# A gated linear attention layer inside a decoder trunk: score blocks over three key tiles instead of chunk states, and a mean square made in one product

## The reference

```
log_a = jax.nn.log_sigmoid(gz @ w_gate_up + b_gate) / 16
b = jnp.cumsum(to_chunks(log_a), axis=3)                # within chunks of 64 tokens
b_ref = b[:, :, :, CHUNK // 2], b_last = b[:, :, :, -1]
scores = einsum('nbhik,nbhjk->nbhij', q * exp(b - b_ref), k * exp(b_ref - b)), causal
o_intra = scores @ v
state = exp(b_last) * state + (k * exp(b_last - b)).T @ v     # from chunk to chunk
o_inter = (q * exp(b)) @ state
o = o_intra + o_inter
o = o * rsqrt(mean(square(o)) + eps) * norm_w; y = o * silu(g); out = y @ w_out
```

## Time and profile before

| | us |
|---|---|
| median of 3 runs | 1059.52 (1059.49 to 1060.53) |
| the profiled execution, device time | 1059.4 |
| its span (first to last instruction) | 1057.7 |
| PE busy | 1038.2 (98%) |
| DVE busy | 728.3 (69%) |
| ACT busy | 521.0 (49%) |
| POOL busy | 131.7 (12%) |

### The profile page before, as it was taken

The page is one execution under the profiler, slowest core; times in us unless marked ns, Lnnn a source line. Parts: engine busy times, 40 slices in busy tenths (PEclk is TensorE's granted clock), DMA queues, the critical chain, the costliest instruction groups (busy, mean ns, idle before and its releaser), DMA issues.

```text
span 1057.7 us, 19726 instructions
## 1 busy us (share of the span) xinstructions
PE 1038.2 (98%) x8195; PEld 1020.7 (97%) x8195; DVE 728.3 (69%) x1100; ACT 521.0 (49%) x758; POOL 131.7 (12%) x146
## 2 busy tenths in 40 slices
PE   7999999999999999999999999999999999999996
PEld 6999999999999999999999999999888999999995
DVE  6765556689789755566796565768745899656644
ACT  4644335465356543344564344447855675444432
POOL 3000002320002000013300000222230220000132
PEclk9999999999999999999999999999999999999997
DMA  7865555637763856556467665662833538765631
GB/s 224 238 196 169 171 165 168 192 98 211 210 176 87 250 172 175 164 165 184 126 197 203 178 173 155 177 172 75 218 92 90 156 95 243 212 183 170 179 92 40
DMA packets 343722, 175.58 MB, mean 166 GB/s; under 512 B 6658, under 2 KB 342576, under 8 KB 343632
## 3 DMA queue, kind: packets, MB, share of 16 engines
q1 hardware_dynamic: 342992, 173.36, 57.6%
q10 hardware_dynamic: 448, 0.85, 0.2%
q0 software_dynamic: 192, 0.10, 0.0%
HBM read 173.24 MB, written 1.05 MB: 165 GB/s over the span
## 4 chain that ended last, share of the span: by engine, by line
PE 93%; DVE 2%; issue 2%; ACT 1%; DMA 1%; POOL 1%; SPq 0%; POOLq 0%; DVEq 0%
PE bank L1209 28%; PE bank L1211 28%; PE bank L1210 28%; PE bank L1234 2%; PE bank L1236 2%; PE bank L1235 2%; DMA raw_weights<-in_ffn_w_in_dram 1%; PE bank L1411 1%; PE bank L1428 1%; ACT weights_hi L427 1%; PE bank L1424 0%; DVE weights_lo L746 0%; PE bank L1437 0%; DVE rstd L862 0%; PE bank L1216 0%
## 5 line engine op out<-in xcount | busy, mean ns | idle before, releaser
L746 DVE TENSOR_TENSOR weights_lo<-raw_weights,weights_hi 128x1024 fp32r<-128x1024 f32 x335 | 415.6, 1246 | 227.3 <-ACT weights_hi L427 226.8
L427 ACT ACTIVATE weights_hi<-raw_weights 128x1024 fp32r<-128x1024 f32 x337 | 355.7, 1059 | 429.7 <-PE bank L1211 372.2
L1209 PE MATMUL bank<-x_hi,weights_hi 128*128 128x272 f32 (+1 forms) x1640 | 474.4, 289 | 0.9 <-ACT kT L629 0.8
L1211 PE MATMUL bank<-x_hi,weights_lo 128*128 128x272 f32 (+1 forms) x1640 | 472.6, 288 | 0.0
L1210 PE MATMUL bank<-x_lo,weights_hi 128*128 128x272 f32 (+1 forms) x1640 | 471.1, 287 | 0.0
L1209 PEld LDWEIGHTS bank<-x_hi,weights_hi 128*128 128x128 f32 x1640 | 310.4, 189 | 4.8 <-issue 2.2
L1211 PEld LDWEIGHTS bank<-x_hi,weights_lo 128*128 128x128 f32 x1640 | 310.6, 189 | 0.0
L1210 PEld LDWEIGHTS bank<-x_lo,weights_hi 128*128 128x128 f32 x1640 | 310.5, 189 | 0.0
L1211 PE MATMUL bank<-mid_hi,weights_lo 128*128 128x272 f32 (+1 forms) x704 | 202.0, 287 | 0.0
L1209 PE MATMUL bank<-mid_hi,weights_hi 128*128 128x272 f32 (+1 forms) x704 | 201.5, 286 | 0.0
L1210 PE MATMUL bank<-mid_lo,weights_hi 128*128 128x272 f32 (+1 forms) x704 | 201.1, 286 | 0.0
(11 more groups left out here) (186 smaller groups left out, 905.1 us busy)
## 6 DMA issues: line engine op xcount, KB each, us to landing
raw_weights<-in_ffn_w_in_dram SPq DMA_DIRECT2D x176, 512.0 KB, 3.9
raw_weights<-in_ffn_w_out_dram SPq DMA_DIRECT2D x64, 512.0 KB, 3.8
raw_weights<-in_ffn_w_out_dram SPq DMA_DIRECT2D x32, 384.0 KB, 3.4
raw_weights<-in_conv_w_in_dram SPq DMA_DIRECT2D x24, 512.0 KB, 3.9
raw_weights<-in_gla_w_in_dram SPq DMA_DIRECT2D x24, 512.0 KB, 3.9
raw_weights<-in_conv_w_out_dram SPq DMA_DIRECT2D x8, 512.0 KB, 4.7
raw_weights<-in_gla_w_out_dram SPq DMA_DIRECT2D x8, 512.0 KB, 4.0
out_dram<-out_tok SPq DMA_DIRECT2D x3, 256.0 KB, 2.2
```

The lines of the kernel that those rows point to most:

```text
L427: nc.scalar.activation(w_hi[:, n % RING, :], raw[:, n % RAW, :], ACT.Copy).then_inc(hi_split, 1)
L746: nc.vector.tensor_tensor(w_lo[:, s, :], raw[:, n % RAW, :], w_hi[:, s, :].bitcast(F32), ALU.subtract).then_inc(lo_split, 1)
L1209: nc.tensor.matmul(ps, w_h, hi[:, k, cols], start=first and k == k0, stop=False)
L1211: mm = nc.tensor.matmul(ps, w_l, hi[:, k, cols], start=False, stop=last and k == k1 - 1)
```

## The change

The chunk states are gone. Tokens are counted in four chunks of 64 from the first meta token (BEFORE = 256) and a rest of 16. Three tiles of keys (128, 128 and 16) meet the queries behind them directly: eight small float32 products make one head's scores (`scores`), with keys that carry the decay to the end of their chunk (`k_late`, POOL, with a second copy one chunk further by DVE) and queries that carry more decay (`q_late`, two small DVE instructions; `late_decays`). Three products per half of the values make the outputs. `turn_k`, `copy_k`, `outers` and `states` are removed. `scores(h)` stands at j = 11 + 2h as before, `outputs(h)` one tile earlier, at 12 + 2h. `decays(h)` stands one tile earlier on ACT.

The mean square is one product with a full 128x128 matrix, so its result stands on all partitions and `spread_rms` is gone. DVE first adds the two halves of the squares (`sum_squares`). Roots and reciprocals are made per head. The last two gate products are on DVE. The four gate logits are made after tile 4, in the middle of tile 5, after it, and in the middle of tile 6, in banks 0 to 3, and tiles 5 and 6 no longer wait for earlier copies.

```diff
 # ACT
-                if j in (9, 11, 13, 15):
-                    decays((j - 9) // 2)
-                if j in (13, 15, 17, 19):
-                    copy_o((j - 13) // 2)
-                if j in (18, 20):
-                    root_ms((j - 18) // 2)
+                if j in (8, 10, 12, 14):
+                    decays((j - 8) // 2)
+                if j in (12, 14, 16, 18):
+                    copy_o((j - 12) // 2)
+                if j == 17:
+                    root_ms(0, 2)
+                    root_ms(2, 1)
+                if j == 19:
+                    root_ms(3, 1)
 # POOL, apply_decays (k_st, q_pos, kT, qT before)
+                nc.gpsimd.tensor_tensor(k_late[:, h % 2, :, 0:3:2, :], k_main, by_last, ALU.mult).then_inc(kst_ready, 1)
...
+                nc.gpsimd.tensor_tensor(q_pos[:, h, :], qT[:, h, :], e_buf[:, 0, META:T], ALU.mult).then_inc(decayed, 1)
...
+                nc.gpsimd.tensor_tensor(qT[:, h, :], qT[:, h, :], e_buf[:, 2, META:T], ALU.mult).then_inc(decayed, 1)
...
+                nc.gpsimd.tensor_tensor(kT[:, h, :], kT[:, h, :], e_buf[:, 1, :], ALU.mult).then_inc(decayed, 1)
-            for m in range(KD):
+            for m in range(KD - 2):
                 gate_output(m)
 # DVE
+            def late_decays(h):
+                dve.wait_ge(exps_ready, 5 * h + 5)
+                dve.wait_ge(kst_ready, h + 1)
+                nc.vector.tensor_tensor(k_late[:, h % 2, :, 1, :], k_late[:, h % 2, :, 0, :],
+                                        decay[:, h, 1:NC:2].rearrange("p (a o) -> p a o", o=1).broadcast_to([P, NC // 2, CH]),
+                                        ALU.mult).then_inc(late_ready, 1)
+                dve.wait_ge(decayed, 3 * h + 2)
...
+                nc.vector.tensor_scalar(q_late[:, h % 2, :], qT[:, h, SEQ - LATE:SEQ], decay[:, h, 2:3], None,
+                                        ALU.mult).then_inc(late_step, 1)
+                dve.wait_ge(late_step, h + 1)
+                nc.vector.tensor_scalar(q_late[:, h % 2, CH:LATE], q_late[:, h % 2, CH:LATE], decay[:, h, 3:4], None,
+                                        ALU.mult).then_inc(late_ready, 1)
+            def sum_squares(h):
+                dve.wait_ge(o_squared, h + 1)
+                if h >= 1:
+                    dve.wait_ge(ms_made, h)
+                nc.vector.tensor_tensor(o_sum[:], o_sq[:, 0, :], o_sq[:, 1, :], ALU.add).then_inc(o_summed, 1)
...
                 if j < GLA_TILES - 1:
                     split_lo(n0 + j + RING)
...
-                if j in (7, 9, 11, 13):
-                    differences((j - 7) // 2)
+                if j in (7, 8, 10, 12):
+                    differences((7, 8, 10, 12).index(j))
+                if j == 8:
+                    nc.vector.memset(sT[:, :, 0, 0:META], 0.0).then_inc(margin_set, 1)
+                if j in (10, 12, 14, 16):
+                    late_decays((j - 10) // 2)
+                if j in (13, 15, 17, 19):
+                    sum_squares((j - 13) // 2)
                 if j in (11, 13, 15, 17):
                     copy_scores((j - 11) // 2)
                 if j == 18:
                     invert_rms(0)
+                    scale_o(0)
+                    invert_rms(1)
+                if j == 19:
+                    scale_o(1)
+                    invert_rms(2)
                 if j == 20:
                     scale_o(2)
+                    invert_rms(3)
                     scale_o(3)
-        Y_CHUNKS = {21: (0, 1), 22: (2, 3), 23: (4, 5), 24: (6, 7)}
+        Y_CHUNKS = {20: (0, 1), 21: (2, 3), 22: (4,), 23: (5,), 24: (6, 7)}
 # PE, scores(h): keys x queries, M x N
+                pe.wait_ge(decayed, 3 * h + 3)
+                pe.wait_ge(late_ready, 2 * h + 2)
+                product(kT[:, h, 0:P], 0, q_pos[:, h, 0:P - META])                                  # 128 x 112
+                product(late[:, 0, 0:CH], CH - META, qT[:, h, CH - META:P - META])                  # 64 x 64
+                product(late[:, 0, CH:3 * CH], P - META, qT[:, h, P - META:P - META + CH])          # 128 x 64
+                product(late[:, 0, CH:3 * CH], P - META + CH, q_late[:, h % 2, :])                  # 128 x 80
+                product(kT[:, h, P:2 * P], SEQ, q_pos[:, h, P - META:2 * P - META])                 # 128 x 128
+                product(late[:, 1, 0:CH], SEQ + CH, qT[:, h, P - META + CH:2 * P - META])           # 64 x 64
+                product(late[:, 1, CH:3 * CH], SEQ + P, qT[:, h, BEFORE - META:SEQ])                # 128 x 16
+                product(kT[:, h, BEFORE:T], SEQ + P + REST, q_pos[:, h, BEFORE - META:SEQ]).then_inc(scores_made, 1)  # 16 x 16
 # PE, outputs(h): per half of the values 256, 144 and 16 columns
+                    nc.tensor.matmul(bank[3][:, first:first + SEQ], v_tok[:, h % 2, 0, v_cols], sT[:, h % 2, 0, META:T],
+                                     start=True, stop=False)
...
 # PE, mean_square(h)
+                pe.wait_ge(o_summed, h + 1)
+                nc.tensor.matmul(bank[1 + h // 2][:, h % 2 * SEQ:(h % 2 + 1) * SEQ], meanV[:], o_sum[:],
+                                 start=True, stop=True).then_inc(ms_made, 1)
...
-                pe.wait_ge(gla_evac, j - 3 if j < 7 else j - 2 if j < 12 else j - 1)
+                if j >= 7:
+                    pe.wait_ge(gla_evac, j - 2)
...
+                middle = (lambda: logits(1)) if j == 5 else (lambda: logits(3)) if j == 6 else None
...
+                if j in (12, 14, 16, 18):
+                    outputs((j - 12) // 2)
+                if j in (11, 13, 15, 17):
+                    scores((j - 11) // 2)
+                if j in (13, 15, 17, 19):
+                    mean_square((j - 13) // 2)
+            pe.wait_ge(gla_evac, GLA_TILES - 1)
```

More of the change, by code:

```diff
@@ L229, in tokens @@
             return slice(T - n, T)
[L232 to L241, removed]
-        def tile_bank(j):
[L244 to L253, removed]
+        def tile_bank(j):
+            return 4 + (j - 3) % 3
         block = ctx.enter_context(nc.Block())
@@ L1137, in invert_rms @@
-            def invert_rms(part):
-                heads = slice(0, 96) if part == 0 else slice(96, P)
-                dve.wait_ge(rms_root, part + 1)
-                nc.vector.reciprocal(rms[heads, :], rms[heads, :]).then_inc(rms_ready, 1)
+                across = SEQ + BEFORE - P + REST
+                dve.wait_ge(margin_set, 1)
+                nc.vector.tensor_copy(sT[:, h % 2, :, :].rearrange("p b t -> p (b t)")[:, META:META + across],
+                                      bank[0][:, 0:across]).then_inc(scores_copied, 1)
@@ L1197, in block_of, with multiply @@
                 return w[:, n % RING, k * P:(k + 1) * P]
-            def multiply(ps, n, source, cols, k0=0, k1=KU, first=True, last=True, ready=None, before_last=None):
+            def multiply(ps, n, source, cols, k0=0, k1=KU, first=True, last=True, ready=None, before_last=None, middle=None):
                 hi, lo = source
@@ L1207, in multiply @@
                         before_last()
+                    if middle is not None and k == (k0 + k1) // 2:
+                        middle()
                     w_h, w_l = block_of(w_hi, n, k - k0), block_of(w_lo, n, k - k0)
@@ L1368, in _, with logits @@
             main = tokens(SEQ)
-            def logits(heads):
-                pe.wait_ge(gla_evac, 1)
+            def logits(h):
+                pe.wait_ge(gla_evac, h + 1)
                 pe.wait_ge(gate_landed, 32)
-                for h in heads:
-                    nc.tensor.matmul(bank[4 + h][:, 0:T], gate_up[:, h * P:(h + 1) * P], gzT[:], start=True,
-                                     stop=True).then_inc(logits_made, 1)
+                nc.tensor.matmul(bank[h][:, 0:T], gate_up[:, h * P:(h + 1) * P], gzT[:], start=True,
+                                 stop=True).then_inc(logits_made, 1)
@@ L1386, in turn_v, with scores @@
+                for b in range(BEFORE // P):
+                    mm = nc.tensor.transpose(bank[7][:, b * P:(b + 1) * P], vT[:, v % 2, b * P:(b + 1) * P], ident[:])
                 mm.then_inc(v_turned, 1)
-            def turn_k(h):
-                pe.wait_ge(kst_ready, h + 1)
+            def scores(h):
+                pe.wait_ge(decayed, 3 * h + 3)
+                pe.wait_ge(late_ready, 2 * h + 2)
+                pe.wait_ge(log_a_ready, 1)
                 if h >= 1:
-                    pe.wait_ge(state_ready, NC * h)
-                for b in range(BLOCKS):
-                    r = slice(0, META) if b == 0 else slice(META + (b - 1) * P, min(META + b * P, KT0))
-                    mm = nc.tensor.transpose(bank[4][0:r.stop - r.start, b * P:(b + 1) * P], k_st[:, h % 2, r], ident[:])
-                mm.then_inc(k_turned, 1)
@@ L1397, in scores @@
[L1397 to L1413 removed]
+                    pe.wait_ge(scores_copied, 2 * h)
@@ new lines, in scores, with product @@
+                ps = bank[0]
+                late = k_late[:, h % 2, :, :, :].rearrange("p a b i -> p a (b i)")
```

(5 more changed lines are left out.)

242 lines of the change are left out of this document (83 added, 159 removed).

## The result

| | before | changed |
|---|---|---|
| median of 6 runs, us | 1060.85 (1059.49 to 1062.18) | 1064.80 (1063.94 to 1068.50) |
| the profiled execution, device time | 1059.4 | 1064.0 |
| its span | 1057.7 | 1062.2 |
| PE busy | 1038.2 | 1033.4 |

The ratio is 1.0045, with a 95% interval of 1.0032 to 1.0059: slower, and clearly more than no change. (The two medians alone differ by 3.95 us, the means of the six runs by 4.7 and the fastest runs by 4.45.) PE has less to do and the kernel lasts longer. The page of the changed kernel shows both, against the earlier trace rows: 4.8 us less busy time, and a chain that lies less on PE (91% after 93%) and more on DVE (4% after 2%) and ACT (2% after 1%).

What follows compares the result with a forecast made beforehand. PE bounds the kernel, busy 98% of the span with 93% of the chain. Front 4.4, middle -1.9, tail 0 and clock 1.7 + 1.2 sum to +5.4 on 1059.4, giving 1064.8 us; range 1060.4 to 1067.0.

Steps and rivals of the forecast that it cites:

- Front, +4.4: Up to tile 12: waits for ACT's copy and DVE's `late_decays(0)` move its start from 762.16 to 766.6; bounds +2.9 to +5.2.
- half clock behind this stop would be hidden: Behind the stop before `turn_v(0)`: tile 11 runs partly at half clock but ends at 763.7, ahead of `scores(0)` at 765.0.
- Middle, -1.9: Tile 12 to the end of tile 18: 38.8 us against 40.7, with stops of 1.25 us at j = 13, 15 and 17.
- `outputs` with 256, 144 and 16 columns, twice, (0.43 + 0.25 + 0.20) x 2 = 1.76: PE's own work: time of the new `outputs` products per head, 1.76 us against the old 2.63.
- The prediction's last sentence: The forecast is wrong if differences or sum come earlier on DVE, or `scores` takes much over 1.9 us, costing in the middle.
- The rival in which the sum is not late: Middle and tail: DVE reaches the sum in time, stops (7.7 us) and half clock behind the last go; 1054.2, chance 0.10.
- Tail, 0: End of tile 18 to the end of `out_projection`'s first chunk: 29.75 us against 29.8; bounds -1.5 to +1.5.
- Clock, +2.9: Half clock after the j = 19 stop (+1.7) and after the first chunk (+1.2, between 0 and 1.7).
- both places that the prediction names: Half clock was forecast in tile 20, behind the 3.9 us stop at j = 19, and from `out_projection`'s first chunk into the next.
- Nearly sure: Tile 20: the 3.9 us stop at j = 19 is followed by half clock, +1.7 us.
- PE's work, 10.5 us less: Whole attention stage: 25.9 us of PE work removed, 4 x 3.85 added, so PE's work falls by 10.5 us.
- the prediction's lower bound of 1.35 us: `scores` per head: 1.35 us if narrow products take only a transpose's 0.11; 1.6 was taken, upper bound 1.67.

Runs made afterwards that it cites:

- e6: Changed kernel with the eight products of `scores` ordered by stationary width (five of 128 columns, two of 64, one of 16): 1066.33 us, ratio 1.0061.
- e1: Changed kernel with the sum of squares ahead of DVE's weight split (heads 0 to 2), head 3's at j = 18 ahead of the second reciprocal: 1060.66 us.
- e12: e4 with unused products as fillers: 2 before `turn_v(0)`, 5 before `turn_v(1)`, 4 before `scores(0)`; 1061.75 us, ratio 1.0021.
- e7: Changed kernel with the logits in two pairs after tiles 4 and 5 again, as before: 1067.17 us, ratio 1.0068.
- e9: e6 on top of e1: sum of squares moved and products grouped, nothing moved in front; 1058.55 us, ratio 0.9983.
- e8: Changed kernel with the moves of e1, e2 and e3 together and the grouped products of e6: 1058.27 us, ratio 0.9981.
- e11: Changed kernel with unused products of 512 columns, 16 before `turn_v(0)` and 12 before `mean_square(3)`: 1067.66 us, ratio 1.0069.
- e2: Changed kernel with ACT's decays one tile later (j = 9, 11, 13, 15), behind the copy `turn_v` waits for: 1069.30 us, ratio 1.0079.
- e3: Changed kernel with `late_decays(0)` on DVE ahead of `split_lo` of j = 9: 1065.85 us, ratio 1.0045.
- e4: Changed kernel with both front edits, those of e2 and e3: 1067.36 us, ratio 1.0063.

## Why the prediction was right, and where not

The forecast of 1064.8 us is the measured median, but some of that is luck: two terms were off in opposite directions, and a third part was in no term. The forecast change was +5.4 us; the profiled executions differ by 4.6, and the medians taken side by side by 3.95. Times at the front are given less the 1.03 us by which the stage starts late.

- **Front, +4.4: right (+4.64), with two small errors that cancel.** The stop before `turn_v(0)` is 4.11 us (4.3 forecast) and ends at 758.46 (758.65). `scores(0)` starts at 764.57 (765.0), `late_decays(0)` takes 0.72 from its first start to its last end (0.6), `scores` 2.23 (1.6). POOL and DVE did hold each other up: the first instruction of `differences(1)` on DVE took 0.95 us at 758.73 beside a busy POOL, and the same one of `differences(2)` 0.41 at 764.02. That half clock behind this stop would be hidden also held.
- **Middle, -1.9: it was -0.50, and the step that failed is "`outputs` with 256, 144 and 16 columns, twice, (0.43 + 0.25 + 0.20) x 2 = 1.76".** It takes 2.28 us (808.02 to 810.30): the 144 columns 0.33, the 16 columns with 16 rows 0.33, and the second half's 256 columns 0.53. Three of these, 0.52 too short each, lie before the end of tile 18: 1.56 us, more than the 1.4 by which the term is off (`mean_square`, 0.35 from its start to the next tile's instead of 0.49, gives a part back). The rest held: `mean_square` comes 3.19 us after the tile's end (776.71 to 779.90, 3.20 forecast), whatever `scores` takes. e6 shows that directly: 775.77 to 778.96 is 3.19 again, with `scores` 0.5 us shorter. The stops are therefore 0.64 us and not 1.25. The prediction's last sentence, by which `scores` of much over 1.9 us would cost in the middle, contradicts its own sum: between `turn_v` and the sum there is room for 3.20 - 0.33 = 2.87 us, and the 2.23 measured cost nothing there.
- **Why it is slower at all: two waits, each of which costs about what PE's saved work is worth.** The forecast put its largest term on the front (ACT's exponentials ahead of the copy, DVE's late decays), and the sum of squares behind the split into the middle and the tail. Both are there. e1 takes off 0.42% (1.0045 to 1.0003), 4.5 us, by the sum's place alone; e12 takes off 0.24%, 2.5 us, at the front alone, with its stops filled. The rival in which the sum is not late did not come true, as the order on DVE forbids it, but e1 makes it true: it is worth the 5.0 - 0.9 us of stops that go, not the 7.7 us that the forecast had.
- **Tail, 0: -0.58, within its bounds**, although `outputs(3)` is 0.52 longer. The stop is 3.10 (3.9) and the chunk ends 0.6 us earlier than forecast behind tile 18.
- **Clock, +2.9: 0 in the profiled run, right in others.** Neither the 3.10 us stop nor the chunk was followed by half clock in it. Without the term the forecast is 1061.9, and 1.03 (late start) + 0.24 + 1.4 - 0.58 make 1064.0, the profiled execution's time. But the runs of the changed kernel differ: three with a mean clock of 0.993 took 1063.94 to 1064.39, the others 1065.21 at 0.990, 1066.62 at 0.989 and 1068.50 at 0.986. The profiled variants have half clock in both places that the prediction names, for 1.4 us (forecast 1.7), for 1.05 (1.2), and for 3.1 to 4.1 where both come (2.9). So the three slower runs most likely hold one or both stretches, which no trace of them can show, and the median, 0.8 us above the profiled one, holds a part of the term. "Nearly sure" was too strong: behind the stop it came in four of seven profiled runs.
- **PE's work, 10.5 us less: 4.8.** `outputs` and `scores` are 0.52 and 0.63 us longer than forecast, four times each: 4.6 us of the 5.7 that are missing.
- **The statement that a weight load lasts in proportion to its stationary columns** (the Trainium skill, "TensorE: Matmul & The Clock Gate", "LDWEIGHTS (loading the stationary operand)") agrees with the trace: the product with 16 stationary columns steps by 0.15 us (767.68 to 767.83), that with 16 rows and 128 columns by 0.33, both with 16 moving columns. The loads themselves (PEld) take 0.11 us for two of 16 columns, 0.29 for two of 16 rows and 128 columns, and 0.30 for two of 128 rows and 128 columns. By itself the page's rule would have put `scores` near the prediction's lower bound of 1.35 us, and 2.23 were measured. Five changes of width at 0.17 us (e6) are 0.87 us, an estimate that about makes up the difference.

**What stays open.** The 1.03 us by which the stage starts late; its start was between 733.5 and 734.9 us in the traces of the variants, so part of it may be chance between executions. Why the median of e7 is higher, and why the clock falls in the tail in some executions and not in others. How often it does in runs without a profile.

## What to carry to other kernels

When work on the busiest engine is replaced by a step through another engine (here a sum on DVE), put that step ahead of the other engine's routine work in its fixed order; otherwise the busiest engine waits for that work, and what it was spared may only lengthen the wait. A stop has a second price behind it, the half clock, and that price may be hidden under a later wait: before removing either wait, follow what comes on the path then, and measure with the gap filled. Price small float32 products from rows of their own shape, and keep those of one stationary width together; that pays only where no wait follows (e6 against e9).

## What the runs showed of the hardware

- The same eight float32 products take 2.15 to 2.23 us with five changes of stationary width between them (e1, the changed kernel) and 1.64 to 1.70 with two (e8, e6): 0.17 to 0.18 us for a change, if the width is the cause.
- A float32 product of 16 rows, 128 stationary and 16 moving columns takes 0.33 us, as long as one of 128 rows with 144 moving columns (808.45, 808.78 and 809.11 of the changed kernel).
- Behind stops of 4.08 and 4.11 us the granted clock was 0.50 and 0.65. Behind a stop of 2.28 us it was 0.50 (e11, from 769 to 771 us). Behind the same stop of 3.10 to 3.13 us it stayed at 1.00 in three profiled runs (the changed kernel, e6, e12) and fell to 0.50 in four (e2, e3, e4, e7). So the length of a stop alone does not tell it.
- The same program ran between 1063.94 us at a mean clock of 0.993 and 1068.50 us at 0.986.
